# B-C products inside a projection, rows ahead of the scores, and two value runs directly behind the scores, in a two-layer hybrid encoder on one core

## The reference

```
proj = h @ w_in ; q, k, v, z, xbc, dt_raw = split(proj)
q, k = rope(q), rope(k) ; attn_out = window_attention(q, k, v, attn_sink)
xbc = silu(depthwise_conv(xbc, ssd_conv_w, ssd_conv_b)) ; xs, bm, cm = split(xbc)
y = bidir_ssd(xs, dt_raw, ssd_dt_bias, ssd_a_log, bm, cm) + ssd_d * xs
ssd_out = rms_norm(y * silu(z), ssd_norm_g)
h = layer_norm(ALPHA * h + concat(attn_out, ssd_out) @ w_out, ln1_g, ln1_b)
gate, val = split(h @ w_up) ; gate = depthwise_conv(gate, ffn_conv_w, ffn_conv_b)
h = layer_norm(ALPHA * h + (silu(gate) * val) @ w_down, ln2_g, ln2_b)
```

## Time and profile before

| | us |
|---|---|
| median of 3 runs | 1298.28 |
| the profiled execution | 1298.11 |
| its span | 1296.3 |
| TensorE matmul busy | 1280.9 |
| VectorE busy | 801.7 |
| ScalarE busy | 609.2 |
| GpSimd busy | 131.0 |
| mean granted TensorE clock | 0.998 |

### The profile page before, as it was taken

How to read it: one execution, slowest core, us unless ns; L and a number is a source line. 1 busy time by engine, 2 the same in 40 slices (tenths; PEclk the granted TensorE clock), 3 DMA queues, 4 the chain that set the end, 5 groups by cost and what they waited for, 6 DMA issues and landing times.

```text
span 1296.3 us, 17993 instructions
## 1 busy us (share of the span) xinstructions
PE 1280.9 (99%) x7456; PEld 1059.5 (82%) x7456; DVE 801.7 (62%) x1071; ACT 609.2 (47%) x913; POOL 131.0 (10%) x125
## 2 busy tenths in 40 slices
PE   9999999999999999999999999999999999999997
PEld 8877778889888888888898777788888888888886
DVE  7888898866444444342378998979654444443425
ACT  5766766436333333311276776653553333332112
POOL 2034511001000000000020354000100000000000
PEclk9999999999999999999999999999999999999999
DMA  5465565423333333323134656563133323223222
GB/s 200 158 147 115 132 146 138 172 77 103 98 98 98 98 98 98 130 98 97 54 127 150 151 114 150 129 179 130 66 114 98 98 98 96 96 93 129 96 95 111
DMA packets 43872, 151.36 MB, mean 117 GB/s; under 512 B 4912, under 2 KB 9424, under 8 KB 42640
## 3 DMA queue, kind: packets, MB, share of 16 engines
q1 hardware_dynamic: 38160, 130.01, 30.2%
q0 software_dynamic: 5632, 20.21, 9.1%
HBM read 141.81 MB, written 6.29 MB: 114 GB/s over the span
## 4 chain that ended last, share of the span: by engine, by line
PE 92%; DVE 6%; ACT 1%; issue 1%; DMA 0%; POOL 0%; SPq 0%; DVEq 0%
PE ps L870 17%; PE ps L871 17%; PE ps L872 17%; PE ps L1028 9%; PE ps L1029 9%; PE ps L1030 9%; PE ps L917 5%; PE ps L1242 2%; DVE cv L1476 2%; PE ps L896 1%; PE ps L1020 1%; DVE ast L1624 1%; PE ps L1189 1%; PE ps L1255 1%; PE ps L1226 1%
## 5 line engine op out<-in xcount | busy, mean ns | idle before, releaser
L870 PE MATMUL ps<-hhi,whi 128*128 128x512 f32 x1040 | 411.2, 395 | 0.9 <-DVE cv L1476 0.7
L871 PE MATMUL ps<-hlo,whi 128*128 128x512 f32 x1040 | 405.5, 390 | 0.0
L872 PE MATMUL ps<-hhi,wlo 128*128 128x512 f32 x1040 | 405.2, 390 | 0.0
L619 ACT ACTIVATE whi<-raw 128x1024 fp32r<-128x1024 f32 x208 | 219.4, 1057 | 214.6 <-DMA raw<-in_units 214.6
L1313 DVE TENSOR_TENSOR wlo<-raw,whi 128x1024 fp32r<-128x1024 f32 x170 | 207.8, 1224 | 149.4 <-ACT whi L619 149.4
L870 PEld LDWEIGHTS ps<-hhi,whi 128*128 128x128 f32 x1040 | 195.4, 188 | 49.3 <-issue 6.7
L872 PEld LDWEIGHTS ps<-hhi,wlo 128*128 128x128 f32 x1040 | 195.5, 188 | 41.3
L871 PEld LDWEIGHTS ps<-hlo,whi 128*128 128x128 f32 x1040 | 195.6, 188 | 39.4
L1028 PE MATMUL ps<-whi,uhi 128*128 128x512 f32 x352 | 137.1, 390 | 0.0
L1030 PE MATMUL ps<-wlo,uhi 128*128 128x512 f32 x352 | 137.0, 389 | 0.0
L1029 PE MATMUL ps<-whi,ulo 128*128 128x512 f32 x352 | 136.9, 389 | 0.0
(11 more groups left out here) (182 smaller groups left out, 1548.7 us busy)
## 6 DMA issues: line engine op xcount, KB each, us to landing
raw<-in_units SPq DMA_DIRECT2D x208, 512.0 KB, 3.5
wlo<-in_units POOLq DMA_DIRECT2D x38, 512.0 KB, 5.5
gb<-in_gb SPq DMA_DIRECT2D x5, 1024.0 KB, 5.5
h_kept<-hb SPq DMA_DIRECT2D x2, 2048.0 KB, 8.9
ha<-h_kept SPq DMA_DIRECT2D x2, 2048.0 KB, 9.6
hb<-in_x SPq DMA_DIRECT2D x4, 512.0 KB, 5.8
v_rep<-v_tm SPq DMA_DIRECT2D x32, 64.0 KB, 2.1
out_y<-hb SPq DMA_DIRECT2D x8, 256.0 KB, 2.0
```

The source lines that it names most:

```text
L619: A(whi[:, m % RING, :], raw[:, m % RING, :], ACT.Copy).then_inc(unit_hi, 1)
L870: mm(out, whi[:, slot, cols], xhi, start=start, stop=False)
L871: mm(out, whi[:, slot, cols], xlo, start=False, stop=False)
L872: return mm(out, wlo[:, slot, cols], xhi, start=False, stop=stop)
```

## The change

The list is reordered. In units 13 to 15 the B-C products and transposes stand ahead of the scores (`T`, `CB` before `AS`). The value runs 0 and 1 leave the middle of units 12 and 14 and stand directly behind the scores of these units. The B-C products 0 and 2 go into the middle of units 13 and 15. On VectorE `PT` goes ahead of `SIL2` in units 9 to 15, and `SC 0` ahead of `SIL2` of block 10. On GpSimd the `MV` steps come earlier. Unit 11 joins the units whose low part is made by the DMA.

PE's work between projections is then: unit 12: AS4, AV0; unit 13 (CB0 in its middle): CB1, T4, AS5; unit 14: T5, AS6, AV1; unit 15 (CB2 in its middle): CB3, T6, AS7.

```diff
-BY_DMA = range(12, 31)
+BY_DMA = range(11, 31)
-AV_AT = {A0 + 4: 0, A0 + 6: 1, A0 + 8: 2, A0 + 9: 3}
+AV_AT = {A0 + 8: 2, A0 + 9: 3}
+AV_END = {A0 + 4: 0, A0 + 6: 1}
+CB_AT = {13: 0, 15: 2}
-        if 0 <= i < 8:
-            steps += [("AS", i), ("AM", i)]
         if i == 8:
             steps += [("PT", 7), ("SIL2", n - 1 - U_CONV), ("XS", n - 1 - U_CONV)]
         j = n - 2 - U_CONV
-        if n in (13, 15):
+        if n in CB_AT:
             steps += [("CB", n - 12)]
         if 4 <= j < N_CONV:
             steps += [("T", j)]
-        if n in (12, 14):
-            steps += [("CB", n - 12)]
+        if 0 <= i < 8:
+            steps += [("AS", i), ("AM", i)]
+        if n in AV_END:
+            steps += [("AV", AV_END[n])]
...
         if 0 <= i < 8:
             steps += [("AX", i)]
+        if n + 1 in CB_AT:
+            steps += [("CB", CB_AT[n + 1])]
...
         if 1 <= i < 8:
-            steps += [("SIL2", n - 1 - U_CONV)]
+            steps += [("PT", i - 1), ("SIL2", n - 1 - U_CONV)]
             if n - 1 - U_CONV >= 4:
                 steps += [("XS", n - 1 - U_CONV)]
-            steps += [("PT", i - 1)]
+        if n == 15:
+            steps += [("MV", 0), ("MV", 1)]
...
             steps += [("SILU", n - U_CONV)]
+            if n == 17:
+                steps += [("SB", 0), ("SC", 0)]
             if not 0 <= i < 8:
                 steps += [("SIL2", n - U_CONV)]
...
-            if n == 17:
+            if n == 16:
                 steps += [("MV", 2), ("MV", 3)]
...
-        if 15 <= n < 17:
-            steps += [("MV", n - 15)]
-        if n == 17:
-            steps += [("SB", 0), ("SC", 0)]
-        elif a >= 0:
+        if a >= 0:
...
+            def mixed(L, i):
+                pe.wait_ge(silu_done, L * N_CONV + 4)
+                wait_aux_free(pe, L, ("CB", i))
+                for g in range(2):
+                    last = mm(ps[:, aux_bank(("CB", i)), g * SEQ:(g + 1) * SEQ], bc[:, g, i * BLK:(i + 1) * BLK],
+                              bc[:, 2 + g, i // 2 * SEQ:(i // 2 + 1) * SEQ], start=True, stop=True)
+                last.then_inc(aux_full, 1)
...
-                        between = functools.partial(values, L, AV_AT[i]) if i in AV_AT else None
+                        between = None
+                        if i in AV_AT:
+                            between = functools.partial(values, L, AV_AT[i])
+                        elif i in CB_AT:
+                            between = functools.partial(mixed, L, CB_AT[i])
                         by_columns(unit(L, i) % RING, unit_bank(i), between)
...
+                    elif what == "CB" and i not in CB_AT.values():
+                        mixed(L, i)
+                    elif what == "AV" and i in AV_END.values():
+                        values(L, i)
```

## The result

The changed kernel takes 1313.70 us (median of 4 runs, 1310.72 to 1316.17); the kernel before 1298.42 (4 runs). The ratio is 1.0119 (95% interval 1.0102 to 1.0136): slower by 15 us, and outside the range given. The four runs lie in two pairs, near 1311 and near 1316; the profiled execution, of the slower pair, took 1316.12 (span 1314.3), 18.0 more than that of before. TensorE executes the same 7456 matmuls.

What follows compares the result with a forecast made beforehand. TensorE, busy 1280.9 of 1296.3 us, was taken as the bound. New waits of 8.5 us less gains of 9.1 gave -0.6; one clock fall (1.7) made it +1.1 on 1298.11, so 1299.2 us, range 1294.6 to 1302.2.

Steps and rivals of the forecast that it cites:

- item 2: Scan's first product behind the transposes: its wait for VectorE's cap goes, gaining 1.95 us over both layers.
- T7: Transposes after unit 15's scan of work: TensorE arrives after 8.9 us, VectorE needs 9.0, so a 0.1 us wait.
- T5: Transposes of unit 14 wait for block 5's SiLU on VectorE: 2.35 us a layer, bounds 1.9 and 2.8.
- scores of block 4: Scores behind unit 12 wait for the exponentials: 0.7 us a layer, bounds 0.2 and 1.2.
- B-C product 0: In mid-unit 13 it waits for the low part from VectorE: 0.3 us a layer, bounds 0 and 0.8.
- T4: Transposes behind unit 13 wait for block 4's SiLU: 0.6 us a layer, bounds 0 and 1.2.
- The SiLU multiply: VectorE's multiply in its new place behind PT: taken at 0.8 us, between 0.69 and 1.11.
- One fall: Clock falls behind unit 14's transposes in one layer, costing 1.7 us; chance 0.33.
- slower rival: Clock falls behind unit 14's transposes in both layers: 1300.9 us, or 1302 with waits at upper bounds; chance 0.24.
- the split of unit 11: Its 1.22 us leave VectorE, so waits at units 10 and 12 go: 0.6 us a layer, 1.2 gained.
- the B-C product's wait: Behind unit 12's scores, the wait for the values' low part goes: 3.6 us gained, if nothing takes its place.

Runs made afterwards that it cites:

- e1: Changed kernel with GpSimd's MV steps back at their old places: 1302.78 us, ratio 1.0030.
- e3: Kernel before with only GpSimd's MV steps moved to their new places: 1304.24 us, ratio 1.0030.
- e5: Changed kernel with one of the two late GpSimd products (MV 3) back in unit 17: 1306.03 us, ratio 1.0051.
- e2: Changed kernel with B-C products and transposes of units 13 to 15 behind the scores again: 1304.24 us, ratio 1.0034.
- c3: Changed kernel with PT behind the SiLU multiply again in units 9 to 15: 1307.46 us, ratio 1.0054.
- c1: Changed kernel with filler products (5.4 us) on TensorE ahead of the wait of unit 14's transposes: 1316.19 us, ratio 1.0124.
- b2_again: Second profile (run of 1296.79 us) of b2: kernel before, B-C product 0 mid-unit 13, first cap ahead of block 10's SiLU; 1295.73 us, ratio 0.9975.
- b4: Kernel before with B-C product 0 mid-unit 13, cap ahead of SiLU, unit 11 by DMA, PT ahead of the multiply: 1297.38 us, ratio 0.9985.
- b5: Kernel before with B-C product 0 mid-unit 13 and unit 11's low part by the DMA: 1297.51 us, ratio 0.9972.
- b1: Kernel before with only B-C product 0 moved to the middle of unit 13: 1293.75 us, ratio 0.9965.
- e4: Changed kernel with MV steps at old places and B-C products and transposes behind the scores again: 1296.14 us, ratio 0.9973.

## Why the prediction was wrong, point by point

**The step that failed.** The prediction named the move of the MV steps only in the change's description and gave it no price; the gain at the cap (item 2) was counted without what runs on GpSimd beside VectorE. Its own row had the clue: the 1.46 us of one SiLU multiply against a least of 0.69. It read this as the length of the instruction. It was a wait: GpSimd's last MV product ends at 150.88, and the multiply 0.56 behind it. The change put two such products onto the multiply of block 9, with the low part and T8 behind it. The cost, from the changed kernel's starts: T8 starts 6.10 us behind the start of unit 17's second half, for 2.88 and 2.85 before, so 3.2 a layer; the fall of the clock behind it adds 0.5 at T8, 0.3 at the scan's product and 2.2 in unit 18, 3.0 a layer. Together 12.4 us for both layers. e1, e3 and e5 show it: undone, alone and halved.

**T7, sized at 0.1, waits 0.77.** Here the prediction looked only at the SiLU. T7 needs the bank of value run 2, and so its low part, which stands on VectorE one step further, behind PT and the multiply. e1 keeps this wait (0.77) and e2, with the rows behind the scores, hasn't got it. From start to start it is 0.93 a layer, 1.7 more than forecast for both.

**T5: mechanism and size right.** 2.35 forecast, 2.32 measured; c3 confirms PT's share. Forecast also right: scores of block 4 (0.7, measured 0.77), B-C product 0 (0.3, 0.34), T4 (0.6, 0.53). The SiLU multiply came to 0.95 in its new place, where 0.8 was taken.

**The clock.** One fall was forecast, at 1.7, and in the profiled execution both layers fell behind T5, 1.5 us each (c1, e1). That is the slower rival's mechanism; it alone gives 1301 and would have stayed in the range. How many layers fall isn't settled by the wait: in e1 one of two did behind the same 2.32 us.

**The gains came.** The cap's wait is gone, the split of unit 11 freed unit 10, the B-C product's wait fell to 0.34. From the forecast of 1299.2 the sum is + 12.4 (T8 and its clock) + 1.7 (T7) + 1.5 (the second fall) + about 1.3 = 1316.1, against 1316.12 profiled. The 1.3 is 0.3 more at block 4's scores, 0.2 at B-C product 0, and 0.8 because T4 and T6 now stand ahead of scores: from their start to the next group it is 0.58 and 0.53 us, where a projection followed after 0.36. Without the T8 term and with one fall the same sum is 1302.2, and e1 measured 1302.78.

**What stays open.** Why a run of values stops after 113 of 128 matmuls in some executions isn't settled: no experiment aimed at it. It was seen in three profiles, b2_again (2.92 us), b4 (2.97) and e3 (1.96). In all three the view of DMA shows the transfer of 0.02 MB on queue 8, the one marked "instruction", in the 2 us behind 112, and it lands 1.4 to 1.5 us before the matmuls go on. b2's first profile, of the same kernel without the stop, has such a transfer between 107 and 109, and b2_again has none from 107 to 112. So the matmuls may have waited for their own instructions; that is argued, not shown, and why the transfer came late stays open. b5's runs, near 1293.2 or near 1297.5, look like the stop too, but its one profile is of the run of 1293.17 and b1's of that of 1293.75, and neither has it. The length of the low clock behind T8 also varies: 6.8 us in the changed kernel, some 3.4 in c1, c3, e2 and e3 behind waits of 1.9 to 3.1. The changed kernel's runs near 1311 have mean clocks of 0.996 and 0.997 and those near 1316 have 0.991, which fits that.

## What to carry to other kernels

When a step moves on one engine, look at what will run beside it on the other engines, here VectorE's multiply beside GpSimd's products: an instruction in the trace that is twice as long as its least form can be a wait in disguise, and the row beside it on GpSimd said here for whom. A reordering of a kernel that is busy 99% on one engine should be taken apart and timed edit by edit: here one of about eight edits, B-C product 0 into mid-projection, measured alone as much gain as any version had (0.35%), and another, GpSimd's, brought most of the loss. Ahead of moving a step that waits (a transpose) in front of one that feeds the other engine (scores), count the other engine's chain from that feed to the awaited result.

## What the runs showed of the hardware

- VectorE's `scalar_tensor_tensor` with both tensor inputs in SBUF stands still beside GpSimd's MV products: 0.69 us alone, 2.15 with one product of 2.2 us, 3.99 with two of 4.07 together. It isn't always held for two. Beside MV 0 and 1 (4.21 together) the multiply of the changed kernel at 140.37 lasts 1.84 and ends 0.55 behind the first of them; the second lasts 2.34 us, and 1.89 with no multiply beside it (before the change, at 144.39), so there it is GpSimd that seems to wait. The same shows before the change: `AN` (two products of 128x512) takes 2.48 us where a multiply gets in between, which lasts 1.11, and 2.03 where the multiply comes later. What lets it in isn't shown. VectorE's PT (one input) lasts 1.23 beside GpSimd, as alone, and the four taps (one input in PSUM) last 3.30 in both cases:

```profile
139.22 1.23 DVE L1660 STREAM_TRANSPOSE p_t<-sc 128x1024 f32<-128x1024 f32 x1
...
140.37 1.84 DVE L1495 SCALAR_TENSOR_TENSOR xsc<-xsc,cv 128x512 f32<-128x512 f32 x1
...
142.14 3.30 DVE L1488 SCALAR_TENSOR_TENSOR cv<-ps,pm,cv 128x508 f32<-128x508 f32 x4
```
```profile
139.77 4.21 POOL L602 TENSOR_TENSOR heads<-cum_a,cn 128x1024 fp32r<-128x1024 f32 x2
```

  The first fence is VectorE in the changed kernel, the second GpSimd in the same stretch. The Trainium skill, "GPSIMD Engine Reference", section Specifications, speaks of contention for instructions with two SBUF inputs; the trace agrees for these three forms, and shows that the contention can be a full halt.
- The granted clock fell from its upper level to its lower one behind idle stretches of TensorE of 3.08 us (both layers of the changed kernel), 2.32 us (both layers there, but one of two in e1), 1.94 and 2.48 us (e3, T8) and 1.73 us (layer 0 of the kernel before, and not behind the same 1.73 us in e3). It did not behind 1.31 us (c3) and 1.50 us (e2, e4), both layers each, nor behind the stop of 2.97 us in b4, and not where filler took the place of the idle stretch (c1). So the length of the idle stretch alone doesn't decide.
- A run of 128 small matmuls can stop for 2 to 3 us with nothing to wait for that the view of waits knows, in three profiles after exactly 113 of them.
